# Splitting the turned heads of the first attention: from ScalarE and VectorE to ScalarE and GpSimd

## The reference

```python
diff_o = _diff_attention(dq, dk, dv, lam, rel_bias)            # 4 heads, values 128 wide
diff_o = _rmsnorm(diff_o, diff_subln[l]) * (1.0 - lam_init)
sb_o = _rmsnorm(_stick_breaking_attention(sq, sk, sv), sb_norm[l])   # 8 heads, 64 wide
mix = jnp.concatenate([diff_o, sb_o], axis=-1) @ w_o[l]
x = x + _rmsnorm(mix, attn_post_norm[l])
```

## Time and profile before

| | |
|---|---|
| median of 3 runs | 1661.89 us (1660.7 to 1662.1) |
| the profiled execution | 1660.71 us, its span 1658.9 us |
| PE busy | 1634.6 us, 99% of the span |
| DVE, ACT, POOL busy | 693.8, 673.8, 753.8 us |
| stretch of the change | 205 to 262 us, PE's granted clock in it 0.50 from about 209.8 to 216.6 us, otherwise 1.00 |

### The profile page before, as it was taken

One profiled execution on the slowest core, in us unless ns is written; L12 is line 12 of the kernel. 1 busy time (PEld: TensorE's weight loads), 2 busy tenths in 40 slices (PEclk: granted clock), 3 DMA queues, 4 the chain that ended last, 5 costly groups with the idle time before them and its releaser, 6 DMA issues.

```text
span 1658.9 us, 21185 instructions
## 1 busy us (share of the span) xinstructions
PE 1634.6 (99%) x8108; PEld 1352.6 (82%) x8108; DVE 693.8 (42%) x1399; ACT 673.8 (41%) x1181; POOL 753.8 (45%) x574
## 2 busy tenths in 40 slices
PE   9999999999999999999999999999999999999997
PEld 7777778888888888888888888888888888888886
DVE  7176655884444226311212225555773311112224
ACT  6355645543334325422223234566573422223322
POOL 7324334564445552744445553643113554444550
PEclk9999999999999999999999999999999999999999
DMA  5411102323223231323322222322002223232231
GB/s 204 145 52 52 41 12 102 110 94 102 92 99 102 89 102 52 126 90 101 101 90 102 96 95 96 96 65 78 27 27 89 89 102 98 93 102 92 99 102 51
DMA packets 42117, 147.37 MB, mean 89 GB/s; under 512 B 4769, under 2 KB 5153, under 8 KB 42017
## 3 DMA queue, kind: packets, MB, share of 16 engines
q1 hardware_dynamic: 40680, 143.39, 26.1%
q10 hardware_dynamic: 1336, 2.63, 0.5%
HBM read 142.84 MB, written 3.41 MB: 88 GB/s over the span
## 4 chain that ended last, share of the span: by engine, by line
PE 82%; DVE 2%; ACT 1%; issue 1%; POOL 1%; DMA 0%; DVEq 0%; ACTq 0%; POOLq 0%
PE PS L525 20%; PE PS L526 20%; PE PS L527 20%; PE PS L1097 5%; PE PS L494 4%; PE PS L1108 3%; PE PS L929 3%; PE PS L501 2%; PE PS L902 2%; PE PS L920 1%; POOL w_lo L569 0%; PE PS L1070 0%; DMA stage<-in_weights 0%; PE PS L547 0%; PE PS L549 0%
## 5 line engine op out<-in xcount | busy, mean ns | idle before, releaser
L569 POOL TENSOR_TENSOR w_lo<-stage,w_hi 128x512 fp32r<-128x512 f32 x524 | 709.7, 1379 | 836.1 <-ACT w_hi L557 835.1
L557 ACT ACTIVATE w_hi<-stage 128x1024 fp32r<-128x1024 f32 x262 | 274.5, 1056 | 511.5 <-DMA stage<-in_weights 511.2
L525 PE MATMUL PS<-H_hi,w_hi 128*128 128x512 f32 x992 | 387.7, 391 | 0.4 <-DVE rcol L1287 0.4
L527 PE MATMUL PS<-H_hi,w_lo 128*128 128x512 f32 x992 | 386.0, 389 | 0.0
L526 PE MATMUL PS<-H_lo,w_hi 128*128 128x512 f32 x992 | 385.9, 389 | 0.0
L525 PEld LDWEIGHTS PS<-H_hi,w_hi 128*128 128x128 f32 x992 | 186.2, 188 | 40.2 <-issue 0.7
L526 PEld LDWEIGHTS PS<-H_lo,w_hi 128*128 128x128 f32 x992 | 186.2, 188 | 39.5 <-issue 1.0
L527 PEld LDWEIGHTS PS<-H_hi,w_lo 128*128 128x128 f32 x992 | 186.2, 188 | 38.6
L525 PE MATMUL PS<-A_hi,w_hi 128*128 128x512 f32 x528 | 205.6, 389 | 0.5 <-DVE A_lo L679 0.5
L527 PE MATMUL PS<-A_hi,w_lo 128*128 128x512 f32 x528 | 205.4, 389 | 0.0
L526 PE MATMUL PS<-A_lo,w_hi 128*128 128x512 f32 x528 | 205.4, 389 | 0.0
(11 more groups left out here) (223 smaller groups left out, 2041.8 us busy)
## 6 DMA issues: line engine op xcount, KB each, us to landing
stage<-in_weights SPq DMA_DIRECT2D x262, 512.0 KB, 3.3
out_t<-Y SPq DMA_DIRECT2D x8, 256.0 KB, 2.0
X<-in_x_t SPq DMA_DIRECT2D x3, 512.0 KB, 7.9
bias_line<-bias_line ACTq DMA_DIRECT2D x1, 1270.0 KB
strip<-bias_line ACTq DMA_DIRECT2D x1, 1024.0 KB, 5.2
stage<-in_weights SPq DMA_DIRECT2D x2, 256.0 KB, 4.6
V<-QF SPq DMA_DIRECT2D x4, 128.0 KB, 2.4
V<-QF SPq DMA_DIRECT2D x4, 127.8 KB, 2.4
```

The lines of the kernel that those rows point to most:

```text
L525: pe.matmul(out, a, h_hi, start=first, stop=False, skip_group_check=skip)
L527: return pe.matmul(out, b, h_hi, start=False, stop=last, skip_group_check=skip)
L557: act.activation(w_hi[:, slot, :], stage[:, slot, :], ACT.Copy).then_inc(hi_done, 1)
L569: lo = pool.tensor_tensor(w_lo[:, slot, cols], stage[:, slot, cols], w_hi[:, slot, cols].bitcast(F32), ALU.subtract)
```

## The change

For the six groups 0 to 5 of the first attention (`SPARED = 6`), ACT copies the turned bank unrounded to one of two float32 buffers `turn_f`, and this copy alone gives bank 7 free (`o_copied`). POOL makes `H_hi` from the buffer with a cast, and then `H_lo` with a subtraction (`pool_turn1`, hooked on POOL at the steps at which DVE's part was hooked). The matmuls of a group wait for `o_pool`. DVE's part goes away for these groups. Groups 6 and 7, and the second attention, stay as they are. `turn_f` lies in room that was free.

```diff
+SPARED = 6
+                turn_f = sb("turn_f", [P, 2, T], ctx=inner)
         def pe_turn1(pe, b, g):
-            if g >= 1:
-                pe.wait_ge(o_split[b], g)
+            if b == 0 and 1 <= g <= SPARED:
+                pe.wait_ge(o_copied, g)
+            elif g >= 1:
+                wait_turned(pe, b, g - 1)
+        def wait_turned(eng, b, g):
+            if b == 0 and g < SPARED:
+                eng.wait_ge(o_pool, g + 1)
+            else:
+                eng.wait_ge(o_split[b], g + 1 - (SPARED if b == 0 else 0))
         def act_turn1(act, b, g):
             act.wait_ge(o_turned[b], g + 1)
-            act.activation(turned(b, g)[0], PS[:, 7, :], ACT.Copy).then_inc(o_hi[b], 1)
+            if b == 0 and g < SPARED:
+                if g >= 2:
+                    act.wait_ge(o_pool, g - 1)
+                act.activation(turn_f[:, g % 2, :], PS[:, 7, :], ACT.Copy).then_inc(o_copied, 1)
+            else:
+                act.activation(turned(b, g)[0], PS[:, 7, :], ACT.Copy).then_inc(o_hi[b], 1)
+        def pool_turn1(pool, g):
+            hi, lo = turned(0, g)
+            pool.wait_ge(o_copied, g + 1)
+            pool.tensor_copy(hi, turn_f[:, g % 2, :]).then_inc(o_pool_hi, 1)
+            pool.wait_ge(o_pool_hi, g + 1)
+            pool.tensor_tensor(lo, turn_f[:, g % 2, :], hi.bitcast(F32), ALU.subtract).then_inc(o_pool, 1)
         def pe_wo1(pe, b, at, groups):
-                pe.wait_ge(o_split[b], g + 1)
+                wait_turned(pe, b, g)
         for g in range(6):
             at = filled(FILL1, 24 * 12 + turn_steps(g)) + 1
             hook(at1, "act0", at, lambda act, g=g: act_turn1(act, 0, g))
-            hook(at1, "dve0", at, lambda dve, g=g: dve_turn1(dve, 0, g))
+            if g < SPARED:
+                hook(at1, "pool", at, lambda pool, g=g: pool_turn1(pool, g))
+            else:
+                hook(at1, "dve0", at, lambda dve, g=g: dve_turn1(dve, 0, g))
```

More of the change, by code:

```diff
@@ L1055, in build @@
         o_split = [sem("o_split1"), sem("o_split2")]
+        o_copied, o_pool_hi, o_pool = map(sem, ("o_copied", "o_pool_hi", "o_pool"))
         def pe_turn1(pe, b, g):
@@ L1078, in turned @@
             return (H_hi[:, k, :], H_lo[:, k, :]) if b == 0 else (T_hi[:, k, :], T_lo[:, k, :])
+        def wait_turned(eng, b, g):
[3 more added lines that the diff above has]
+                eng.wait_ge(o_split[b], g + 1 - (SPARED if b == 0 else 0))
         def act_turn1(act, b, g):
             act.wait_ge(o_turned[b], g + 1)
-            act.activation(turned(b, g)[0], PS[:, 7, :], ACT.Copy).then_inc(o_hi[b], 1)
+            if b == 0 and g < SPARED:
[10 more added lines that the diff above has]
+            pool.tensor_tensor(lo, turn_f[:, g % 2, :], hi.bitcast(F32), ALU.subtract).then_inc(o_pool, 1)
         def dve_turn1(dve, b, g):
             hi, lo = turned(b, g)
-            dve.wait_ge(o_hi[b], g + 1)
+            dve.wait_ge(o_hi[b], g + 1 - (SPARED if b == 0 else 0))
             dve.tensor_tensor(lo, PS[:, 7, :], hi.bitcast(F32), ALU.subtract).then_inc(o_split[b], 1)
```

## The result

The changed kernel takes 1667.35 us (median of 6 runs, 1666.05 to 1669.26) against 1661.3 us for the kernel before (6 runs, 1659.83 to 1662.1). The ratio is 1.0038, 95% interval 1.0028 to 1.0048: slower by 6.3 us, with bounds of about 4.7 and 8.0 (the medians alone differ by 6.05). Forecast were +6.7 us and 1668.6 us, range 1664.8 to 1671.6.

What follows compares the result with a forecast made beforehand. PE was taken as the bound, 99% busy, so its waits count. A 4.6 us wait plus 2.4 clock loss minus 0.3 gain, +6.7 on 1661.9, gave 1668.6 us, range 1664.8 to 1671.6.

Steps and rivals of the forecast that it cites:

- The wait at group 4: PE waits 4.6 us before group 4's matmuls, as POOL's pair stands behind a weight unit waiting for ACT's rounding.
- Cast and subtraction: POOL's work per group: cast 0.61 us, subtraction 1.27 us, 0.1 us between them, 1.98 us in all.
- The clock: PE's clock falls in the wait at group 4 and stays low after it; 2.1 to 2.6 us, taken 2.4.
- The gain: At group 1's transposes PE's 0.97 us lead shrinks to about 0; an earlier clock rise saves 0 to 0.7, taken 0.3.
- Group 1: POOL done at 217.7 us, behind the scaling; PE wants it at 218.57 us, so hidden with 0.8 us of cover.
- DVE beside POOL: DVE instructions with two SBUF inputs may be delayed by POOL's new work, but cost PE nothing: 0.
- The sum: Wait 4.6 plus clock 2.4 minus gain 0.3 gives +6.7 us; own range +5.0 to +8.2.
- The rivals: Four alternatives: wait without clock loss (0.08), slower POOL (0.08), gain decides (0.04), small wait under 3.3 us net (0.04).
- Rival 2: POOL slower than the rows say, cast 1.27 us, or POOL and DVE obstruct each other; +8.4 to +10.3 us, chance 0.08.
- rival 3: The gain decides, at most 3.0 us faster, only if ACT's rounding ran 4.6 us earlier, making group 4 timely; chance 0.04.

Runs made afterwards that it cites:

- experiment 1: Changed kernel with POOL's two low-half instructions of step 46's weight unit moved behind groups 4 and 5; 1660.21 us, ratio 0.9997 to the kernel before.
- experiment 5: Changed kernel with POOL's two low-half instructions of step 46's weight unit moved between groups 4 and 5; 1663.62 us, ratio 1.0015 to the kernel before.
- experiment 9: Changed kernel with ACT's rounding of the weight unit moved from step 46 to step 43, POOL's queue unchanged; 1659.54 us, ratio 0.9996 to the kernel before.
- experiment 3: Changed kernel with only groups 0 to 4 on POOL, group 5 split by ACT and DVE as before; 1668.31 us, ratio 1.0046 to the kernel before.
- experiment 4: Changed kernel with 20 filler matmuls on PE in front of group 4's matmuls, where it would wait; 1664.92 us, ratio 1.0025 to the kernel before.
- experiment 6: On top of experiment 1, the scaling of the sixth head group moved behind POOL's pair for group 1; 1659.94 us, ratio 0.9993 to the kernel before.
- experiment 10: Experiment 6 with group 5 back on ACT and DVE, plus 7 filler matmuls in PE's step 41 pause; 1660.34 us, ratio 0.9995 to the kernel before.
- experiment 2: Changed kernel with only groups 0 to 3 on POOL, 4 and 5 split by ACT and DVE as before; 1659.72 us, ratio 0.9997 to the kernel before.
- experiment 8: Kernel before with 7 filler matmuls in PE's pause of 1.64 us at step 41; 1660.04 us, ratio 0.9998 to the kernel before.
- experiment 7: Kernel before with ACT copying six groups to the float32 buffer and making the high half, DVE the low, POOL nothing; 1660.38 us, ratio 0.9997.

## Why the prediction was right, by its own steps

- **The wait at group 4**: predicted 4.6 us for the order in POOL's queue, measured 4.59 us. The chain has the predicted members. Experiments 1, 5 and 9 show the cause from three sides: the unit behind the groups (no wait at group 4), between them (2.50 us, at group 5), ahead of them but not waiting (none). Experiment 3 shows that group 5 has no part in it.
- **Cast and subtraction**: 0.61 us taken from the cast from integers, measured 0.61 us in five of six; the subtraction 1.26 to 1.29 us for 1.27.
- **The clock**: a fall with the wait, as predicted, but the working behind the size failed. It took the fall 3.2 us after PE went idle and a low stretch of 6.8 us. In the profile after, the clock fell 4.6 us after PE went idle (227.2 us), as PE resumed, and was low for 3.4 us; in that of experiment 3 it fell 2.7 us after (228.95 us) and was low for 6.8 us, of which PE worked some 4.6. Taken were 2.4 us of price; against experiment 4 from group 5's transposes on the two cost 1.5 and 2.1 us, and experiment 4 gives 2.2 us by ratios. So the term was too large by 0.2 to 0.9 us.
- **The gain** is the step that was argued wrongly. The prediction let PE's lead shrink to about 0 by 215.24 us, since the transposes there were said to need DVE's L1017, done at 215.20 us. In the profile after PE makes these transposes at 212.79 us, 1.5 us before that DVE instruction even begins (there L1019, 214.28 us); they need the one of the step before. Nor does the product with V ahead of them wait for ACT's copy L974: it starts at 211.57 us, ahead of that copy (212.08 us), and waits 0.51 us for DVE's L995. What does hold PE is L995 again at 215.25 us (1.02 us) and then POOL. A lead of 0.9 us is left at group 5's transposes, and 1.4 us in experiments 6 and 10, where the wait for POOL is gone too. Taken were 0.3 us, all of it clock. Experiments 1, 2, 6 and 9, without the wait at group 4, give -0.5 to -1.2 us by their ratios with intervals that hold 0. Experiment 2 shows that the lead isn't the clock's.
- **Group 1** was taken as hidden with 0.8 us of cover. POOL was done at 217.56 us, as worked out (217.7), but PE came 1.4 us earlier than in the profile before, and waited 0.46 us. The step that failed is the cover: it was counted from the old time of PE, as if the change left that alone. It follows from the same wrong lead of 0. Full clock isn't needed for it: with the clock low from 209.8 to 213.2 us experiment 2 has the wait of 0.44 us too, and the kernel before with full clock until 217.5 us (experiment 8) reaches group 2's transposes only 0.2 us sooner than it did (9.88 us after group 0's for 10.06), the changed kernel 2.4 us sooner (7.63). How PE would have come with 6.8 us of low clock in the changed kernel wasn't seen.
- **DVE beside POOL** was put at 0. DVE's instruction with two SBUF inputs (229.08 us) ran into group 4's cast, which took 0.82 instead of 0.61 us: 0.2 us on the path, which is inside the measured 4.59 us. That the wait still came out to a hundredth is in part luck: the 0.2 us was made up by the weight unit (2.49 us for 2.53), by the cast's record, which begins 0.07 us before the unit's ends, and by how the wait is counted. From the time at which PE began these matmuls without a wait, as the prediction counted, it would be 4.66 us.
- **The sum**: +6.7 against +6.3 (4.7 to 8.0) measured. The wait, its main term, was right by its mechanism. The two small terms both err to the same side: by the profiles the terms are 4.6 + 1.5 - 0.9 = +5.2 us for the stretch (5.1 measured). That the times lie 6.3 us apart, nearer to the forecast, may come from clock changes that the working doesn't hold: a longer low stretch behind the wait (0.6 us more in experiment 3's profile) and the one in the second attention (1.5 us) are candidates; which executions have them isn't shown. So that 6.7 is this close is in part luck. The forecast's own range of +5.0 to +8.2 doesn't come out of its bounds either: they give 4.6 + 2.1 - 0.7 = +6.0 to 5.2 + 2.6 = +7.8, or +8.4 with group 5.
- **The rivals**: none came. Rival 2's obstruction is there with 0.2 us, and rival 3's condition was made in experiment 9, with a gain that can't be told from nothing.

## What to carry to other kernels

Work given to an idle engine goes to a place in its queue, and what counts is what stands ahead of it there and whom that waits for: POOL was idle for 5.0 us, had group 4's data for the last 3.8 of them (ACT's copy, 222.78 + 0.59 us), and PE waited 4.6 us all the same. When a hook or a step is added, write out the queue around it, and look at the waits of the rows ahead, not only at their work. And a cover read from the old trace shrinks when the change itself brings the waiting engine forward: before a wait is used as a pin, check by the step which instance of an instruction it is for.

## What the runs showed of the hardware

- With the same pause of 1.64 us at step 41 the clock fell in some executions and not in others: low for 6.8 us from 209.8 us in the profile before, 3.4 us from 209.3 to 210.2 us in experiments 2, 4, 6 and 7, 3.4 us from 217.7 us in experiments 3 and 9, and not at all around this place in the profile after and in experiments 1 and 5. With the pause filled the clock was low from 217.5 us in experiment 8 and not at all in experiment 10. After the wait of 4.59 us it fell both times.
- After the wait of 2.50 us (experiment 5) it was low for 3.4 us too. The part from group 5's transposes on is 4.1 us longer than before, which is 2.5 of wait and 1.6 of clock; the lead of 0.9 us takes off from it, and by ratios the loss was 2.5 us.
- The loss on sharing between DVE and GpSimd falls on either side: the cast took 0.82 us beside DVE's instruction with two SBUF inputs and 0.61 us alone; `pool_lo` at 223.41 us (experiment 9) took 2.97 us for 2.5. In the same run DVE's instruction at 227.00 us took 1.70 us beside POOL's subtraction, where it took 0.62 us alone (225.42 us in the profile after); PE had no wait by it.
